# Gate projections by seven half-size products a group, all gates and branch projections behind the last head, in a hybrid encoder

## The reference

```
h = rms_norm(x, ln_g) * (1.0 + scale[:, None, :]) + shift[:, None, :]
...
for i, y_i in enumerate((ya, yb, yc)):
    z = cols(COL_Z + i * BRANCH_WIDTH, BRANCH_WIDTH)      # h @ w_in[:, ...], 1024 -> 512
    g = cols(COL_G + i * D_MODEL, D_MODEL)                # h @ w_in[:, ...], 1024 -> 1024
    u = jax.nn.sigmoid(g) * ((y_i * jax.nn.silu(z)) @ w_br[i])   # 512 -> 1024
    merged = u if merged is None else merged + u
out = merged @ w_out
return x + gate[:, None, :] * out
```

## Time and profile before

| | |
|---|---|
| time, median of 3 runs | 2394.0 us (2393.01 to 2395.01) |
| the profiled execution | span 2391.6 us |
| PE busy | 2354.4 us, 98% of the span |
| DVE, ACT, POOL busy | 1403.5, 1032.6, 58.6 us |
| PE's granted clock, mean | 0.999 of full speed |

### The profile page before, as it was taken

How to read it: one execution, slowest core, us unless ns; L and a number is a source line. 1 busy time by engine, 2 the same in 40 slices (tenths; PEclk the granted TensorE clock), 3 DMA queues, 4 the chain that set the end, 5 groups by cost and what they waited for, 6 DMA issues and landing times.

```text
span 2391.6 us, 41156 instructions
## 1 busy us (share of the span) xinstructions
PE 2354.4 (98%) x15754; PEld 2120.3 (89%) x15754; DVE 1403.5 (59%) x4033; ACT 1032.6 (43%) x2835; POOL 58.6 (2%) x103
## 2 busy tenths in 40 slices
PE   7999999999999999999999999999999999999999
PEld 5888888988899999888888888898988999998888
DVE  7876425775356676543478853277643676765432
ACT  5666314663134444432356662256522444444220
POOL 0010001200000000000001000021000000000000
PEclk9999999999999999999999999999999999999999
DMA  7221222112111111321420111212121111122123
GB/s 276 95 72 36 80 80 94 35 49 84 56 64 39 51 54 58 115 83 48 159 82 34 45 45 66 74 34 63 52 71 62 44 55 59 56 82 89 67 68 123
DMA packets 50931, 173.48 MB, mean 73 GB/s; under 512 B 8240, under 2 KB 21168, under 8 KB 48304
## 3 DMA queue, kind: packets, MB, share of 16 engines
q1 hardware_dynamic: 40800, 157.70, 19.0%
q10 hardware_dynamic: 9936, 13.15, 1.7%
HBM read 162.44 MB, written 6.29 MB: 71 GB/s over the span
## 4 chain that ended last, share of the span: by engine, by line
PE 90%; DVE 4%; ACT 3%; DMA 1%; issue 1%; SPq 0%; DVEq 0%; ACTq 0%
PE ps_proj L780 75%; PE ps_score L926 2%; PE ps_pt L939 2%; PE ps_pv L975 2%; PE ps_score L910 1%; PE ps_pv L956 1%; PE ps_tr L990 1%; PE ps_tr L991 1%; PE ps_pv L969 1%; ACT act_hi L1183 1%; DMA w_raw<-in_w 1%; DVE top L1678 1%; PE ps_score L916 1%; PE ps_proj L828 0%; PE ps_score L828 0%
## 5 line engine op out<-in xcount | busy, mean ns | idle before, releaser
L780 PE MATMUL ps_proj<-w_hi,act_hi 128*128 128x384 f32 x1824 | 632.6, 347 | 3.3 <-ACT act_hi L1183 2.1
L780 PE MATMUL ps_proj<-w_hi,act_lo 128*128 128x384 f32 x1824 | 612.1, 336 | 0.0
L780 PE MATMUL ps_proj<-w_lo,act_hi 128*128 128x384 f32 x1824 | 611.7, 335 | 0.0
L780 PE MATMUL ps_proj<-act_hi,w_hi 128*128 128x256 f32 (+1 forms) x1312 | 443.5, 338 | 0.0
L780 PE MATMUL ps_proj<-act_lo,w_hi 128*128 128x256 f32 (+1 forms) x1312 | 441.7, 337 | 0.0
L780 PE MATMUL ps_proj<-act_hi,w_lo 128*128 128x256 f32 (+1 forms) x1312 | 441.1, 336 | 0.0
L780 PEld LDWEIGHTS ps_proj<-w_hi,act_hi 128*128 128x128 f32 x1824 | 342.8, 188 | 9.1 <-ACT act_hi L1183 5.7
L780 PEld LDWEIGHTS ps_proj<-w_lo,act_hi 128*128 128x128 f32 x1824 | 343.4, 188 | 0.0
L780 PEld LDWEIGHTS ps_proj<-w_hi,act_lo 128*128 128x128 f32 x1824 | 342.5, 188 | 0.0
L1273 ACT ACTIVATE sig<-ps_proj 128x512 f32<-128x512 f32 (+1 forms) x144 | 70.5, 490 | 501.6 <-PE ps_proj L780 500.1
L1869 DVE TENSOR_TENSOR w_lo<-w_raw,w_hi 128x1536 fp32r<-128x1536 f32 (+3 forms) x169 | 272.5, 1613 | 19.5 <-ACT w_hi L1107 19.1
(11 more groups left out here) (202 smaller groups left out, 3393.6 us busy)
## 6 DMA issues: line engine op xcount, KB each, us to landing
w_raw<-in_w SPq DMA_DIRECT2D x128, 768.0 KB, 4.5
w_raw<-in_w SPq DMA_DIRECT2D x40, 512.0 KB, 3.9
w_ada<-in_w_mod SPq DMA_DIRECT2D x11, 1536.0 KB, 6.7
first_ada<-in_w_first SPq DMA_DIRECT2D x8, 1024.0 KB, 13.0
out_y<-merged ACTq DMA_DIRECT2D x16, 256.0 KB, 2.0
merged<-in_x_in SPq DMA_DIRECT2D x8, 384.0 KB, 6.1
x_old<-in_x_in ACTq DMA_DIRECT2D x8, 256.0 KB, 4.1
out_y<-merged ACTq DMA_DIRECT2D x16, 128.0 KB, 3.6
```

The costliest lines, as they stand in the source:

```text
L780: op = pe.matmul(out, sta[s](k), mov[m](k), start=(k == 0 and n == 0), stop=(k == chunks - 1 and n == 2))
```

## The change

The gate projection of two blocks of 128 output columns (a group) is no longer made of 4 quarter blocks in 8 half-size products but of 7 (Strassen's scheme, in its form with 4 weight sums T1 to T4 and 4 input sums S1 to S4). A product (`s` unit) is 12 matmuls of 384 columns, 4 chunks of 128 by three high and low parts. Four `b` units of 12 matmuls of 384 columns follow; the 12 groups of a layer come behind the last head, C first, then A, then B. Only `z` stays where it was for A and B; the gated y of A and B is parked in DRAM (`park`) and fetched again (`load_back`).

- SP loads the four quarters of a group's gate weights (W12, W11, W22, W21: 256 KB each) and one branch piece (`wb_raw`, 512 KB) in place of a piece `m` of 768 KB.
- POOL makes T1 to T4 (`combos`, 128x512) and, once a layer, S1 to S4 in ten operations of 128x1536 (`mixes`).
- ACT copies seven high parts of 128x512, the branch's of 128x1024, saves two products from PSUM (`keep`) and makes four sigmoids.
- DVE writes the low parts, adds the products up in five additions of 128x384 (`add_up`), and merges.

The diff, cut to what the text speaks of:

```diff
@@ -78,25 +105,27 @@
-    gates_and_merge("C")
+    swish("C")
+    for kind in MERGE_ORDER:
+        for j in range(SUPER):
+            out.extend(("s", l, kind, j, i) for i in range(len(PRODUCTS)))
+            out.extend(("b", l, kind, j, m) for m in range(len(BLOCKS)))
     out.extend(("o", l, 2 * f + half) for f, half in OUTPUTS)
...
+PRODUCTS = (("R", "T1", "S1"), ("P", "W11", "X11"), ("Q", "T2", "S2"), ("R", "W22", "S4"), ("Q", "T3", "S3"),
+            ("P", "W21", "X12"), ("Q", "T4", "X22"))
+MIX_LO_AT = {5: "S1", 6: "S2", 7: "S3"}
+    _late = _p[0] == "z" and _p[2] == "C" or _p[0] == "a" and _p[2] == ADA_GROUPS[_p[1]] - 1
+    _b = min((2, 3) if _late else range(RING), key=lambda b: LAST_USE[_held[b]] if _held[b] else -1)
...
+            def load_quarters(g):
+
+                before = group_before(g)
+                n = ALL_GROUPS.index(g)
+                for q in QUARTERS:
...
+                        if before:
+                            sp.wait_ge(*proj_ready.at(product(before, q)))
...
+                    sp.dma_start(dst[:], w_gate[n, :, at]).then_inc(*quarter_in[q].inc(g))
+
+            def load_branch(g):
...
+                if n >= 2:
+                    sp.wait_ge(*proj_ready.at(("b", *groups_of(g[0])[n - 2], 3)))
...
+            def load_groups(l):
+                for g in groups_of(l):
+                    if group_before(g):
+                        load_quarters(g)
+                    load_branch(g)
+                    if g[2] == 0 and g[1] in PARKED:
+                        load_back(l, g[1])
...
+                if i == 4:
+                    pe.wait_ge(*summed.at((g, "U2")))
+                if i == 5:
+                    pe.wait_ge(*kept_ready.at((g, "M1")))
+                if i == 6:
+                    pe.wait_ge(*summed.at((g, "U3")))
...
+                if u1 is not None and u1[0] == "s":
+                    if u1[4] < 2:
+                        keep(u1)
+                    elif u1[4] > 2:
+                        sigmoid(u1)
...
+                    if g[1] in PARKED and g[2] == 0 and at in (5, 6):
+                        for k in (2 * at - 10, 2 * at - 9):
+                            back_high(l, g[1], k)
+                    if not last_group(g):
+                        if at == 3:
+                            branch_high(group_after(g))
+                        for c in HI_AT.get(at, ()):
+                            s_high(group_after(g), c)
...
+            def add_up(u):
...
+                if u[4] == PLACE["T3"]:
+                    dve.wait_ge(*proj_ready.at(u))
...
+                    dve.tensor_tensor(sum3[:], sum_bank(u), kept1[:], ALU.add).then_inc(*summed.inc((g, "U3")))
...
+                    if not last_group(g):
+                        if at == 4:
+                            branch_low(group_after(g))
+                        for c in LO_AT.get(at, ()):
+                            s_low(group_after(g), c)
```

More of the change, by code:

```diff
@@ L79, in head, with swish @@
                 out.append(ada.pop(0))
-    def gates_and_merge(kind):
+    def swish(kind):
         out.extend(("z", l, kind, n) for n in range(8))
-        for n in range(16):
-            out.extend((("g", l, kind, n), ("b", l, kind, n)))
     for h in range(HEADS):
@@ L117, in bank_key, with groups_of, group_before, group_after @@
         return ("score" if joint(u) else "turned", AT[u] % 2)
+    if u[0] == "s":
+        return ("sum", PRODUCTS[u[4]][0])
     return ("proj", AT[u] % 2)
+def groups_of(l):
+    return [(l, kind, j) for kind in MERGE_ORDER for j in range(SUPER)]
+ALL_GROUPS = [g for l in range(DEPTH) for g in groups_of(l)]
+def group_before(g):
+    n = groups_of(g[0]).index(g)
+    return groups_of(g[0])[n - 1] if n else None
+def group_after(g):
+    n = groups_of(g[0]).index(g)
+    return groups_of(g[0])[n + 1] if n + 1 < len(groups_of(g[0])) else None
+def last_group(g):
+    return group_after(g) is None
+def product(g, w):
+    return ("s", *g, PLACE[w])
 BEFORE_IN_BANK, _banks = {}, {}
@@ L375, in build @@
         y_tok = sb("y_tok", [P, P])
[L377 to L380, removed]
+        mix_at.append(t_at["probs_t"])
+        sq_new = [sb(f"sq_new{b}", [P, 512], F32, mix_at[5] + 4 * 512 * b) for b in range(3)]
+        sq_sum = [sb("sq_sum_p", [P, SEQ], F32, t_at["crossed"]), sb("sq_sum_s", [P, DEC], F32, t_at["probs1"] + 4 * 128)]
@@ L381, in build @@
+        part = [sb(f"part{b}", [P, HALF], F32, t_at["probs0"] + 4 * HALF * (3 + b)) for b in range(2)]
+        sig_of = {(0, 1): sum2, (1, 1): sum3, (0, 0): sig11, (1, 0): kept1}
+        parked = nc.dram_tensor("parked", (DEPTH * len(PARKED), P, HK, TOK), F32, kind="Internal").ap()
         ident = sb("ident", [P, P])
@@ L881, in mean_squares @@
                 pe.wait_ge(*sq_added.at((l, last_square(l, half))))
[L882 removed]
+                pe.matmul(ps_pt[:, half * 512:half * 512 + n], ones[:], sq_sum[half][:], start=True, stop=True
                           ).then_inc(*ms_ready.inc((l, half)))
@@ L2035, in _weights @@
         w[at, :, :part.shape[1]] = part
-    return w
+    w_gate = np.zeros((len(ALL_GROUPS), P, 4, HK, P), np.float32)
+    w_branch = np.zeros((len(ALL_GROUPS), P, HK, 256), np.float32)
+    for n, (l, kind, j) in enumerate(ALL_GROUPS):
+        b = "ABC".index(kind)
+        for c in range(2):
+            full = _strip(w_in[l], g0 + b * D + (2 * j + c) * P)
+            w_gate[n, :, c], w_gate[n, :, 2 + c] = full[:, :HK], full[:, HK:]
+        w_branch[n] = _strip(w_br[l, b], 256 * j, 256)
+    return w, w_gate, w_branch
 def kernel(x_prompt, x_sample, c_prompt, c_sample, ln_g, w_ada, b_ada, w_in, qn_a, kn_a, lam_q1, lam_k1, lam_q2,
```

501 lines of the change are left out of this document (412 added, 89 removed).

## The result

The changed kernel takes **2673.8 us** (median of 4 runs, 2670.7 to 2677.4) against 2394.5 us before: 1.117 of it, 95% interval 1.1153 to 1.1184, **11.7% slower**. The forecast was 2613 us with a range of 2536 to 2675. The direction and the mechanism were as forecast. The profiled execution has a span of 2667.1 us, 275.5 more than before, where the sum had +219.

The account below looks back on a forecast made before the run. The prediction took PE, busy 98% of the span, as the bound. Its terms, -45 + 172 + 34 + 13 + 15 + 30 = +219 us, gave 2613 us, 9% slower, with a range of 2536 to 2675.

Parts of the forecast that it names:

- the signs that the prediction named: Profile after: PE near 90% busy, 22 waits of 7 to 8.5 us before the seventh product, POOL's mixes near 3.9 us.
- the third rival: Group wait comes, and clock stays half twice as long or POOL blocks DVE for whole operations: 2647 to 2683 us, chance 0.10.
- removed matmuls: Gates and branches: 528 matmuls of 384 columns replace 576 a layer, six times, -45 us.
- wait before product 6: Groups: product 6 waits for U3, queued behind the branch piece's late load; 22 x 7.8 = +172 us.
- half clock behind these waits: PE after each group wait: one 3.4 us stretch at half clock loses 1.55 us, 22 times, +34 us.
- POOL's input sums: C's first head: each of ten POOL operations a layer catches one DVE operation half-way; 2 x 15 = +30 us.
- entry to the groups: Start of C's groups: late z pieces and S4 make PE wait 3.4, 1.1 and 2.8 us; 2 x 7.3 = +15 us.
- parked branches: First group of A and of B: first b unit's chunks wait about 3.2 us; 4 x 3.2 = +13 us.
- start of the outputs: Last merge, high and low part need about 4 us, PE reaches that chunk after 4.8; added at nothing.
- the upper bound in the text: POOL's sums each delay a DVE operation by a whole operation: 33 us a layer, 66 in all.
- the milder reading: POOL's sums catch DVE operations half-way, 30 us, instead of near 66 by the skill's rule of full blocking.
- The other side: Chains from load to U3 and at the entry are hidden behind PE's work: 2349 us, chance 0.05.

Follow-up runs that it names:

- run 7: Changed kernel with branch piece loaded first and used later, POOL's input sums spread, entry low parts reordered, parked branch's parts earlier: 2365.2 us.
- run 1: Changed kernel with the next group's branch piece loaded ahead of the four quarters, not behind W21: 2455.8 us.
- run 2: Changed kernel with the load left last, but ACT's high part of the branch piece at place 10 and DVE's low part at place 1 of the next group: 2454.0 us.
- run 5: Changed kernel with the branch piece loaded between W22 and W21, two products earlier: 2571.7 us.
- run 8: On top of run 7, DVE makes U3 six times in a row, to delay it by a set time: 2410.7 us.
- run 9: On top of run 7, DVE makes U3 nine times in a row, to delay it by a set time: 2497.0 us.
- run 3: Changed kernel with each of POOL's ten input sums a layer made as four additions of 128x384, back to back: 2648.7 us.

## Why the prediction was right, and where its sizes were off

The mechanism was right, and the signs that the prediction named came: PE 89% busy, 22 waits before the seventh product for U3 (21 of them 7.8 to 8.3 us, one 8.9), ACT and DVE idle for the branch piece. Only POOL's sums took 3.5 us and not 3.9. That the time lies inside the range is partly luck. The loss was 275.5 us where the sum had 219, and nearly all the errors go the same way. The range's upper end, 2675, was set inside the third rival's 2647 to 2683 without a sum of its own.

The terms, beside what they measured in the profiled execution. A gap costs its idle time and 0.16 us of overlap more. Matmuls at half clock lose 1 - 0.1746 / 0.32 = 0.455 of their time.

| term | predicted, us | measured, us |
|---|---|---|
| removed matmuls | -45 | -49.5 (0.1733 in place of 0.1746 each, run 7) |
| wait before product 6 | 22 x 7.8 = 172 | 178.0 + 22 x 0.16 = 181.5 |
| half clock behind these waits | 34 | 108 us at half clock x 0.455 = 49 |
| POOL's input sums | 30 | 54.3 + 4 x 0.16 in four gaps, 7 of half clock: 62 |
| entry to the groups | 15 | 12.7 + 6 x 0.16 in six gaps, 3 of half clock: 17 |
| parked branches | 13 | 2.8 + 4 x 0.16 = 3.5 |
| start of the outputs | 0 | 3.4 + 4 x 0.16 in four gaps, 1.6 of half clock: 5.6 |
| sum | +219 | +269 |
| span | | +275.5 |

Some six microseconds are left over: 2 of them are idle time in small gaps, and the rest was not followed up.

- **The wait before product 6** was right step by step. Runs 1 and 2 show that it comes from two queues together, run 5 that the chain behind the load is fixed. Only the load was longer, 4.86 us from issue to ACT's start (4.6 to 5.0 in all 22) where I took 4.3; the other steps are within 0.05 us.
- **The removed work** was right in kind. That a run of 24 matmuls takes 4.19 us includes the last one's overlap, so 0.1746 was 1% too much.
- **The clock** was the right mechanism. I took one stretch of 3.4 us behind each wait, by the earlier trace rows. By the granted clock the stretches behind the waits were 2.8 to 6.2 us, 4.9 on average, so 2.2 us lost each and not 1.55.
- **POOL's input sums** are the step that failed: "if each of the ten catches one DVE operation half-way". Each caught one near its beginning. DVE's next operation of the kind that is held stands ready when the POOL operation starts, so it is late by most of that operation's length. That was near the upper bound in the text, 33 a layer, and the measured waits are 27.4 and 26.9 a layer, with POOL's operations 3.5 us long and not 3.9. The clock behind these gaps was not in the term. The rule of the Trainium skill (SBUF — State Buffer, SBUF: two separate sides) quoted beside the term was right, and my sum went by the milder reading.
- **Parked branches** cost 3.5 us, not 13, since the late product 6 covered them. Run 1 took the cover away, and the term came out at 11.9 us of gaps and 9 of half clock: 21 us. These gaps are as long as the forecast ones; the clock was not in the term.
- **The entry** was right to 0.5 us in each of its three waits: 3.2, 0.9 and 2.3 us against 3.4, 1.1 and 2.8. The half clock behind the first of these was not in the term.
- **The start of the outputs** was counted as covered, with 4.8 us for a chain of about 4. PE waited 1.1 and 0.6 us a layer.

The rivals: the one with the clock low for longer and POOL blocking for whole operations (0.10, 2647 to 2683 us) was nearest. The other side, 2349 us, was not reached by the change, but run 7 comes to 2365 us with the same arithmetic once the orders are mended. The scheme saves PE 49.5 us, and in the change they were bought with losses of 325 us (275.5 + 49.5), more than six times as much.

## What to carry to other kernels

When units get shorter, walk the next group's loads through every in-order queue: a load nobody needs yet does harm as soon as a copy that waits for it stands ahead of something urgent. Either issue it before the waits of its neighbours or take the copy out of the urgent part of the queue; both gave the same 218 us. Work moved to POOL isn't free beside DVE: here each POOL operation of 3.5 us delayed one DVE operation by 2.2 to 3.3 us, so spread such operations out, one at a time, where DVE has that much slack. Packing them or only cutting them smaller leaves much of the price. And price a wait of PE from about 2 us upwards at up to 2 us more than its length, also where two shorter waits that stand close together come to that.

## What the runs showed of the hardware that was not expected

- PE's clock behind short waits in otherwise dense work: after 1.5 to 1.7 us of idle time it stayed at 2.4 GHz in 21 of 21 cases (run 8), after 2.8 us it fell in 2 of 3 (run 8), in run 9 (3.3 us at most places) in 23 of 24, and after 3.8 us (run 5) and 8.1 us (the changed kernel) in all 22. Between these it goes both ways: a gap of 2.2 us behind one of 0.7 (run 1, above) and a single one of 2.1 us (run 7, at the entry to the groups) were followed by half clock; one of 2.3 us at the entry (the row with issue, above) was not in the changed kernel and was in one layer of run 5; the one of 2.0 us in the earlier trace rows was not.
- Two waits close together can do it as well. At the start of the outputs PE waits 1.1 us and, about 1 us after it has gone on, 0.6 us more. The granted clock fell to half within 0.6 us behind the second one in 8 of the 20 cases of the changed kernel and the nine runs. From PE's timeline in the changed kernel, layer 2:

```profile
2599.43 0.39 PE L1034 MATMUL ps_proj<-act_lo,w_hi 128*128 128x512 f32 x1
...
2600.64 0.80 PE L1034 MATMUL ps_proj<-act_hi,w_hi 128*128 128x512 f32 x1 [0.59 <-DVE act_lo L2270]
2601.24 0.63 PE L1034 MATMUL ps_proj<-act_lo,w_hi 128*128 128x512 f32 x1
```

- The Trainium skill (TensorE: Matmul & The Clock Gate, Why this matters for your kernels) warns of gaps over about 3 us. The runs agree at 3.3 us, and show falls also behind a single gap of 2.1 us and behind the two of 1.1 and 0.6.
- The time at half clock behind a wait hardly depends on its length: 4.2 us on average behind 3.3 us of idle time, 4.3 behind 3.8, 4.9 behind 8.1. Single stretches are 2.8 to 6.2 us.
- A POOL addition of 128x384 took 1.09 us in run 3, where 128x1536 took 3.5, that is 0.87 for a quarter. Most of the difference is a fixed part of each operation: from 1.28 us for 512 columns (the weight sums) and 3.42 for 1536 an estimate for 384 is 1.0, and the shortest piece took 0.99. Whether waiting for DVE makes up the rest isn't shown for these pieces; two of the eighty, beside a DVE operation of 1536 columns, took 2.5 us.
